# Encoder block on one core: the end of the output projection and the first MLP units in another order (squares beside the gate, residual in halves, diagonals ahead of the residual, four x1 chunks turned first and twelve between MLP units)

## The reference

```python
o = jnp.concatenate([rms_norm(o_a, g_out_a[l]), rms_norm(o_b, g_out_b[l])], axis=-1)
o = o @ w_out[l]                                   # (512 x 2048) @ (2048 x 2048)
x = x + gt_a * rms_norm(o, g_post_attn[l])         # this is x1

h = rms_norm(x, g_pre_mlp[l]) * (1.0 + sc_m) + sh_m   # this is h2
y = jnp.square(jax.nn.relu(h @ w_mlp_in[l])) @ w_mlp_out[l]
x = x + gt_m * rms_norm(y, g_post_mlp[l])
```

## Time and profile before

| what | value |
|---|---|
| median of 3 runs | 2155.28 us |
| lowest and highest | 2152.96 and 2156.47 us |
| the profiled execution's own time | 2155.57 us |
| span of its trace | 2153.9 us |
| TensorE matmuls busy | 2083.9 us, 97% |
| VectorE, ScalarE, GpSimd busy | 1503.6, 857.3, 74.5 us |
| end of the output projection's last matmul | 784.98 us |
| first matmul of MLP unit 0 | 802.83 us |
| mean granted TensorE clock | 0.989 of full |

### The profile page before, as it was taken

One profiled execution on the slowest core, in us unless ns is written; L12 is line 12 of the kernel. 1 busy time (PEld: TensorE's weight loads), 2 busy tenths in 40 slices (PEclk: granted clock), 3 DMA queues, 4 the chain that ended last, 5 costly groups with the idle time before them and its releaser, 6 DMA issues.

```text
span 2153.9 us, 26797 instructions
## 1 busy us (share of the span) xinstructions
PE 2083.9 (97%) x9410; PEld 1721.4 (80%) x9410; DVE 1503.6 (70%) x1827; ACT 857.3 (40%) x1178; POOL 74.5 (3%) x85
## 2 busy tenths in 40 slices
PE   5999999999899989999999999999999999999997
PEld 5788888877788868888888888888788888888886
DVE  6786898778877765644454445543889889888866
ACT  5444322578842343322332233322433333333322
POOL 0000000011100000000000000002000000000000
PEclk8999999999999999999999999999999999999999
DMA  9986869600077644666556655676765467456441
GB/s 318 284 286 222 284 204 255 191 30 1 30 262 255 217 173 137 234 228 201 185 200 227 207 184 193 227 251 194 280 250 211 146 228 261 140 216 240 175 176 78
DMA packets 214206, 435.17 MB, mean 202 GB/s; under 512 B 30164, under 2 KB 69752, under 8 KB 205304
## 3 DMA queue, kind: packets, MB, share of 16 engines
q1 hardware_dynamic: 195992, 361.43, 50.2%
q0 software_dynamic: 16704, 67.11, 8.7%
q10 hardware_dynamic: 1440, 5.70, 0.7%
HBM read 367.09 MB, written 67.11 MB: 202 GB/s over the span
## 4 chain that ended last, share of the span: by engine, by line
PE 80%; DVE 7%; DMA 4%; ACT 4%; issue 4%; DVEq 0%; SPq 0%; ACTq 0%; POOLq 0%
PE bank L1988 11%; PE bank L1989 11%; PE bank L1990 11%; PE bank L2354 7%; PE bank L2356 7%; PE bank L2355 7%; PE bank L1976 4%; PE bank L1978 4%; PE bank L1977 4%; DMA raw<-in_w_ada 2%; PE bank L2401 1%; PE bank L2403 1%; PE bank L2402 1%; PE bank L2033 1%; PE bank L2034 1%
## 5 line engine op out<-in xcount | busy, mean ns | idle before, releaser
L1218 DVE TENSOR_TENSOR lo<-raw,hi 128x1024 fp32r<-128x1024 f32 (+2 forms) x236 | 278.4, 1183 | 391.0 <-ACT hi L716 389.1
L716 ACT ACTIVATE hi<-raw 128x1024 fp32r<-128x1024 f32 (+2 forms) x236 | 239.3, 1023 | 656.2 <-PE bank L1990 417.8
L1988 PE MATMUL bank<-h_hi,hi 128*128 128x512 f32 x1024 | 399.0, 390 | 3.5 <-DVE h_lo L1739 3.5
L1990 PE MATMUL bank<-h_hi,lo 128*128 128x512 f32 x1024 | 398.4, 389 | 0.0
L1989 PE MATMUL bank<-h_lo,hi 128*128 128x512 f32 x1024 | 398.4, 389 | 0.0
L2354 PE MATMUL bank<-hi,y_use 128*128 128x512 f32 x784 | 306.6, 391 | 8.1 <-DVE acc L1883 3.8
L2356 PE MATMUL bank<-hi,y_use 128*128 128x512 f32 x784 | 305.2, 389 | 0.0
L2355 PE MATMUL bank<-lo,y_use 128*128 128x512 f32 x784 | 305.0, 389 | 0.0
L1161 ACT ACTIVATE hi<-w 128x1024 fp32r<-128x1024 f32 x168 | 178.3, 1062 | 295.3 <-PE bank L2356 217.6
L1807 DVE TENSOR_TENSOR lo<-w,hi 128x1024 fp32r<-128x1024 f32 x168 | 204.1, 1219 | 38.1 <-ACT hi L1161 37.3
L1988 PEld LDWEIGHTS bank<-h_hi,hi 128*128 128x128 f32 x1024 | 192.3, 188 | 43.6 <-DVE h_lo L1739 3.7
(11 more groups left out here) (295 smaller groups left out, 3089.8 us busy)
## 6 DMA issues: line engine op xcount, KB each, us to landing
raw<-in_w_ada SPq DMA_DIRECT2D x192, 512.0 KB, 4.9
raw<-in_w_mlp_in SPq DMA_DIRECT2D x128, 512.0 KB, 4.1
w<-in_w_mlp_out SPq DMA_DIRECT2D x128, 512.0 KB, 5.2
y_dram<-y_out POOLq DMA_DIRECT2D x32, 1792.0 KB, 7.8
y_use<-y_dram SPq DMA_DIRECT2D x53, 1024.0 KB, 8.8
raw<-in_w_in SPq DMA_DIRECT2D x32, 512.0 KB, 5.7
raw<-in_w_out SPq DMA_DIRECT2D x32, 512.0 KB, 4.9
raw<-in_w_in SPq DMA_DIRECT2D x48, 256.0 KB, 5.1
```

The costliest lines, as they stand in the source:

```text
L716: ins = nc.scalar.activation(dst, src, ACT.Copy)
L1218: ins = tt(dst, src, high.bitcast(F32), ALU.subtract)
L1988: mm(acc[n][:], wh, act_hi[:, k, :], start=first and q == 0, stop=False)
L1990: ins = mm(acc[n][:], wl, act_hi[:, k, :], start=False, stop=last and q == QROWS - 1)
```

## The change

ScalarE's `square` of the last column block waits for the sum, not for the gate, and writes its squares to PSUM bank 2 or 3 in place of `part`. The residual is done in two halves of 1024 columns, and so are ScalarE's squares of x1; the DMA that saves x1 is issued behind them. VectorE does the diagonal of the tile before ahead of the residual, with an addition of the two half sums. Both splits of MLP unit 0 move to the end of tile 2's part of the loop. TensorE turns four chunks ahead of the MLP instead of eight, all into banks 4 to 7, once all four sums are done; the other twelve are turned in three blocks ahead of units 1, 3 and 5. Unit 0 waits for two chunks of h2 in place of four. Nothing of the table `FIRST_AFTER` is changed.

```diff
@@ ScalarE
+            def square_last(t):
+
+                act.wait_ge(b_sum, (NB - 1) * 4 + t + 1)
+                if t == 0:
+                    act.wait_ge(mod_read, MODS + 4)
+                if t >= 2:
+                    act.wait_ge(row_done, (NB - 1) * 4 + t - 1)
+                nc.scalar.activation(bank[2 + t % 2][:], part[:, t, :], ACT.Square, accum_out=row_sq[:, t, NB - 1:NB]).then_inc(row_done, 1)
+
             for t in range(NT):
-                square(NB - 1, t)
-                root(max(2 * t, 1), t, 0)
-                if t == NT - 1:
+                square_last(t)
+                if t:
+                    root(2 * t, t - 1, 1)
+                root(2 * t + 1, t, 0)
+                for half in range(2):
+                    act.wait_ge(x1_ready, 2 * t + half + 1)
+                    cols = slice(half * HALF, (half + 1) * HALF)
+                    nc.scalar.activation(z_tok[:, t, cols], x_res[:, t, cols], ACT.Square, accum_out=stat[:, t, 1 + half:2 + half]).then_inc(x1_sq, 1)
+                act.dma_start(x1_d[t], x_res[:, t, :]).then_inc(x1_saved, 16)
+                if t == NT - 2:
                     split_hi(*at_mlp(0, 0))
-                if t:
-                    root(2 * t + 1, t - 1, 1)
-                act.wait_ge(x1_ready, t + 1)
-                act.dma_start(x1_d[t], x_res[:, t, :]).then_inc(x1_saved, 16)
-                nc.scalar.activation(z_tok[:, t, :], x_res[:, t, :], ACT.Square, accum_out=stat[:, t, 1:2]).then_inc(x1_sq, 1)
             root(2 * NT, NT - 1, 1)
...
-                    src, g, b = bank[k if k < 8 else 4 + k % 4][:], gsc_m[:, k:k + 1], shf_m[:, k:k + 1]
+                    src, g, b = bank[4 + k % 4][:], gsc_m[:, k:k + 1], shf_m[:, k:k + 1]
@@ VectorE
             def diagonal(t):
 
-                dve.wait_ge(x1_sq, t + 1)
+                dve.wait_ge(x1_sq, 2 * t + 2)
+                own.step(tt(stat[:, t, 1:2], stat[:, t, 1:2], stat[:, t, 2:3], ALU.add))
                 ts(stat_v[:, t, 1:2], stat[:, t, 1:2], 1.0 / D, EPS, ALU.mult, ALU.add).then_inc(x1_var, 1)
-                dve.wait_ge(x1_sqrt, min(2 * t + 3, 2 * NT))
+                dve.wait_ge(x1_sqrt, 2 * t + 2)
...
-                stt(x_res[:, t, :], z_tok[:, t, :], rstd[:, t, 0:1], x_res[:, t, :], ALU.mult, ALU.add).then_inc(x1_ready, 1)
+                for half in range(2):
+                    cols = slice(half * HALF, (half + 1) * HALF)
+                    stt(x_res[:, t, cols], z_tok[:, t, cols], rstd[:, t, 0:1], x_res[:, t, cols], ALU.mult, ALU.add).then_inc(x1_ready, 1)
...
                 sum_tile(NB - 1, t)
                 gate_tile(NB - 1, t)
-                residual(t)
                 if t:
                     diagonal(t - 1)
-            split_lo(*at_mlp(0, 0))
+                residual(t)
+                if t == NT - 2:
+                    split_lo(*at_mlp(0, 0))
             diagonal(NT - 1)
@@ TensorE
+            pe.wait_ge(b_sum, 4 * NB)
             for t in range(NT):
                 pe.wait_ge(xn_ready, t + 1)
-                for k in range(8):
-                    if t == 0 and k == 4:
-                        pe.wait_ge(z_done, 4 * NB)
-                    ins = turn_x1(k, t, bank[k])
+                for k in range(4):
+                    ins = turn_x1(k, t, bank[4 + k])
                     if t == NT - 1:
                         ins.then_inc(xn_turned, 1)
+            pe.wait_ge(row_done, 4 * NB)
...
-                if j in (2, 4):
-                    pe.wait_ge(h2_ready, 4 + 2 * j)
-                    for k in range(4 + 2 * j, 8 + 2 * j):
+                if j in (1, 3, 5):
+                    pe.wait_ge(h2_ready, 2 * j + 2)
+                    for k in range(2 * j + 2, 2 * j + 6):
                         for t in range(NT):
                             ins = turn_x1(k, t, bank[4 + k % 4])
                         ins.then_inc(xn_turned, 1)
-                pe.wait_ge(h2_ready, max(4, 2 * j + 2))
+                pe.wait_ge(h2_ready, 2 * j + 2)
```

More of the change, by code:

```diff
@@ L1711, in residual @@
                 ts(stat_v[:, t, 0:1], stat[:, t, 0:1], 1.0 / D, EPS, ALU.mult, ALU.add).then_inc(x1_var, 1)
-                dve.wait_ge(x1_sqrt, max(2 * t, 1))
+                dve.wait_ge(x1_sqrt, 2 * t + 1)
                 own.step(nc.vector.reciprocal(rstd[:, t, 0:1], stat_s[:, t, 0:1]))
                 dve.wait_ge(res_landed, 16 * (t + 1))
-                stt(x_res[:, t, :], z_tok[:, t, :], rstd[:, t, 0:1], x_res[:, t, :], ALU.mult, ALU.add).then_inc(x1_ready, 1)
+                for half in range(2):
+                    cols = slice(half * HALF, (half + 1) * HALF)
+                    stt(x_res[:, t, cols], z_tok[:, t, cols], rstd[:, t, 0:1], x_res[:, t, cols], ALU.mult, ALU.add).then_inc(x1_ready, 1)
             for t in range(NT):
@@ L1733, in _ @@
                     k1 = k + 1
-                    ts(h2_f32[k1 % 4][:], bank[k1 if k1 < 8 else 4 + k1 % 4][:], gsc_m[:, k1:k1 + 1], shf_m[:, k1:k1 + 1],
+                    ts(h2_f32[k1 % 4][:], bank[4 + k1 % 4][:], gsc_m[:, k1:k1 + 1], shf_m[:, k1:k1 + 1],
                        ALU.mult, ALU.add).then_inc(h2_mid, 1)
```

## The result

The changed kernel takes 2158.99 us in the median of 12 runs (2157.5 to 2167.32), the kernel before, run beside it, 2154.56 us in the median of 12 (2150.46 to 2159.88). The ratio is 1.0023 with a 95% interval of 1.0015 to 1.0031, that is 5.0 us slower (3.2 to 6.7). Forecast was 5.2 us more than the profiled execution of before, 2160.8 us, a ratio of 1.0024 to that execution. "The projection" is from here on the output projection, and its end the end of its last matmul.

The account below looks back on a forecast made before the run. TensorE was taken as the bound in the MLP's up projection. Start -2.5, third block +3.5, wait ahead of unit 5 +2.2 and clock +2.0 made +5.2 on 2155.57: 2160.8 us, range 2156.6 to 2164.0.

Parts of the forecast that it names:

- Unit 0's start: From the output projection's end to MLP unit 0: quicker loop and turns start it near 800.3 instead of 802.83, -2.5 us.
- Moving unit 0's split: VectorE's split between residual 2 and sum 3 waits for ScalarE's split; the 1.3 us won are given back.
- Third block: Turns moved from TensorE's wait ahead of unit 0 into the never-idle MLP stretch: three blocks instead of two, +3.5 us.
- The wait ahead of unit 5: TensorE waits behind the last block for unit 5's split, still made after chunk 13 of that block: +2.2 us.
- The clock: Idle TensorE ahead of unit 0 lets it start at the lower clock, 4 us at that level: +2.0 us.
- The square's PSUM destination: ScalarE's square of the last column block writing PSUM: bounded at plus or minus 0.15 us per tile, taken as nothing.
- the forecast's last sign: Prediction wrong if the stretch from unit 0 to unit 8 is not longer by about 5.7 us plus the clock.
- the held clock: Rival: clock stays at 2.4 GHz through unit 0, then +3.2 us, 2158.8 us; chance 0.19.
- the start without gain: Rival: half squares, addition and PSUM destination cost more, unit 0 starts no earlier: +7.7, 2163.3 us; chance 0.06.
- The second dip behind unit 5's wait: Rival: clock dips again after that wait, or first dip longer: 1.4 to 3.4 us more, 2162.2 to 2164; chance 0.17.
- The faster one: Rival: chunks, splits and loads pace the first MLP group, hiding third block and wait; only -2.5, 2153.1 us; chance 0.08.

Follow-up runs that it names:

- e2: Changed kernel with MLP unit 0's splits back in the last tile, VectorE's behind the last residual; ratio to the kernel before 1.0006.
- e6: Changed kernel with the first block of turns between MLP units (chunks 4 to 7) done twice; one run, unit 5 starts 60.78 us after the projection.
- e1: Changed kernel with unit 5's weights split after chunk 11 instead of chunk 13; ratio to the kernel before 1.0007.
- e4: Changed kernel with unread matmuls (20, 18 and 9) in TensorE's three idle stretches ahead of unit 0; ratio to the kernel before 1.0012.
- e3: Kernel before with only the new loop over tiles, squares into spare SBUF, unit 0's split late, turns nearly as before; ratio to the kernel before 0.9991.
- e7: Changed kernel with unit 5 split after chunk 11, unit 0's splits in the last tile, and unread matmuls ahead of unit 0; ratio to before 0.9988.
- e8: e3 with 10 repeated turns behind tile 2's and 8 unread ones once chunk 0 of h2 is made; ratio to the kernel before 0.9980.
- e5: Kernel before with only TensorE's part and banks of the change, first turns waiting for all four sums; ratio to the kernel before 1.0023.

## Why the prediction was right

By its own steps, with the changed kernel's trace:

- **Unit 0's start, forecast -2.5.** Measured -2.63, and the idle of VectorE ahead of the first `split_lo` was 2.16 us, forecast about 2. The residuals stood where they were forecast: counted from the end of the projection at 784.98 they were to come at -13.9, -7.6, -2.0 and 7.1 us, and came at -13.89, -7.63, -2.02 and 6.97. Moving unit 0's split cost what was said, and e2 shows the other half of it: without that the start would have come 3.07 us earlier still.
- **Third block, forecast +3.5.** The rows show 3.5, and e6, which doubles one, 3.57 on the path.
- **The wait ahead of unit 5, forecast +2.2.** The trace has an idle of 2.08, counted from the end of the block's last matmul (837.59). Counted as the forecast did, from where the next matmul could have started, 3.49 us into the block, it is 2.31 (839.66 less 837.35). It was released by the split that was named, and e1, which takes it away, gains 2.34.
- **The clock, forecast +2.0 from bounds 0 and 3.4.** Unit 0 lasted 7.67 us in place of 5.60: +2.07. e4 shows the cause. This was the softest term, an estimate from the one dip of the rows, and that it came out so close is in part luck. e1 and e6 have the changed kernel's code up to there, and unit 0 took 7.65 us in the one and 6.93 in the other. The way to the dip was not quite the one forecast either: 4.6 us of idle were to stand ahead of the fourth diagonal, and there were 1.86, because the clock had fallen before the first turns already and the turns of tiles 0 to 2 took 5.19 us.
- **The square's PSUM destination, taken as nothing.** It took 0.60 us (at 766.57), where one into SBUF takes 0.63, at 768.41 in e3 and at 770.25 in the earlier trace rows: 0.03 us, far inside the bound of 0.15. The accumulator read, which the root waits for, began 0.54 us after the square's start in both (767.11, and 768.95 in e3), so none of it was on the path. The Trainium skill's sentence ("ScalarE: Activation LUTs", Step-by-step) has the sign right; over four tiles it comes to a tenth of a microsecond, not the tenths that I read into it.

Together the four, as measured, are -2.63 + 3.49 + 2.31 + 2.07 = 5.24 of the 5.25 us at unit 5. From unit 0 to unit 8 the stretch is 7.97 us longer (58.82 against 50.85), that is 5.7 and 2.27 for the clock, as the forecast's last sign asked. Two slips in the working change nothing of this: the held clock less the scatter, 2158.8 less 2.6, is 2156.2 and not the 2156.6 at which the range begins, and the 32 and 64 "calls" of the section on the clock are matmul records, two to a call. Of the rivals, the held clock and the start without gain didn't occur. The second dip behind unit 5's wait didn't either. The faster one, that chunks and splits pace the first group, is refuted by e6. What neither the sum nor the ratio separates is the part of the clock elsewhere. The spans differ by 3.8 us though the change's stretch started 2.95 us earlier and took 5.25 longer, so 1.5 us were lost behind it. The changed kernel's profiled execution had further dips at 1553 and 2126 us. The traces bear out that these are the place: from unit 5's start to the end of the span it is 1316.1 to 1316.5 us in the three traces that have neither dip (before, e7, e8), 1317.5 to 1318.0 in the five with one of them (e1, e2, e3 and e5 the later one, e6 the earlier), and 1318.0 and 1319.4 in the two with both (the changed kernel and e4). Whether the change brings them on or chance does stays open; no run was made for it. Against the change speaks that e3, with the turns of before, has one too, and that the 27 executions of the kernel before beside e4 go from 0.985 to 0.991 in mean granted clock.

## What to carry to other kernels

Where one engine is busy without a gap, look at what work a change carries across the edge of that stretch: moving four chunks' turns out of the wait ahead of unit 0, and waiting for two chunks of h2 in place of four, gave 2.72 us (e5), and the same turns cost all of their 3.5 us behind it. A table that spaces one engine's work by another's order, as the splits by chunks, must move with that order. And a wait in an in-order program is priced by what stands behind it, not by what it waits for: the split of unit 0 cost 3 us in one place, and nothing behind the last residual, where VectorE waits for ScalarE's squares: the next step, the addition, started 0.02 us after ScalarE's last read had ended, in e2 as in the changed kernel.

## What the runs showed of the hardware

Matmuls whose result nobody reads, put into idle stretches, cost nothing that the traces show and kept the clock up: with the same start of unit 0 within 0.02 us, e4 ran unit 0 in 5.53 us at a granted clock of 1.00 where the changed kernel took 7.67 at 0.5 for most of it. The Trainium skill ("TensorE: Matmul & The Clock Gate", Why this matters for your kernels) warns of idle gaps between bursts of matmuls, and these traces agree: the three kernels filled in this way (e4, e7, e8) have no wait of TensorE above 0.73 us between the projection and unit 0 and no dip there, and the other seven have longer waits and each a dip. What I had not expected is that the kernel with only the quicker loop would have a dip too: e3's unit 0 started at full clock behind a wait of 2.29 us, shorter than the 3.48 us of the earlier trace rows behind which the clock held, and the clock fell within the unit and gave back 1.6 of the 3.57 us won. A shorter wait is thus no promise, and a gain on such a path is to be read together with the clock of what follows.

ScalarE's issue of the x1 save (ACTq, its instruction queue), put behind the squares, starts 0.01 us after the second square has started and runs beside it. ScalarE after, and below it ScalarE before:

```profile
770.65 1.06 ACT L1094 ACTIVATE z_tok<-x_res 128x1024 f32<-128x1024 f32 x1
770.66 0.34 ACTq L1095 DMA_DIRECT2D x_dram<-x_res  x1
```

```profile
774.20 0.34 ACTq L1085 DMA_DIRECT2D x_dram<-x_res  x1
774.60 1.92 ACT L1086 ACTIVATE z_tok<-x_res 128x2048 f32<-128x2048 f32 x1 [3.01 <-DVE x_res L1715]
```

In the order before it stood ahead of the square, which began 0.4 us after the issue had (and after the residual had ended, 774.17).
